# Identity products on TensorE ahead of 12 places of a two-block transformer kernel

## The chip, the cores and the metric

One core of a Trainium2 chip runs the whole program in one launch. The metric is the device time of that launch in microseconds (us), the median of several runs. All data are float32.

## The reference, cut to what matters

256 tokens of width 1024 pass through two layers of a first block (compressed, selected and windowed attention, a gated linear recurrence and a 31-tap convolution side by side) and then through one layer of a second block (latent attention, a chunked recurrent mixer, and a product-key expert layer).

```
for l in range(2):                                   # the first block
    proj = rms_norm(x, norm_g[l]) @ w_in[l]
    q, k_c, v_c, ..., u_lru, z_lru, glu_a, glu_b, z_conv = split(proj)
    y_nsa  = nsa_attention(rope(q), ..., compress: silu(blk @ cmp_w1) @ cmp_w2)
    y_lru  = rg_lru(u_lru, ...)
    y_conv = conformer_conv(glu_a, glu_b, ...)       # 31 taps, norm, @ w_pw2
    x = x + concat(y_nsa*silu(z_nsa), y_lru*silu(z_lru), y_conv*silu(z_conv)) @ w_out[l]
x = rms_norm(x, final_g)
# the second block: sh, sc, gt come from silu(c) @ w_ada
h = rmsnorm(x)*(1+sc1)+sh1;  x = x + gt1 * (concat(mla(h), mlstm(h)) @ w_out)
h2 = rmsnorm(x)*(1+sc2)+sh2
# experts: 8 heads x 16 rows of a table of 16384, chosen per token by two top-16 lists
x = x + gt2 * sum_k gelu(expert_u[e_k] . h2) * g_k * expert_v[e_k]
```

## The kernel before, in words

Every engine has its own instruction list, written out by hand, and events (semaphore counts) tie the lists together. TensorE runs through `first_tensor` for layer 0 and 1, `mix_tensor` (the mixers of the second block), and `peer_tensor` (the experts).

In `first_tensor` the projections come first. Then a loop over 20 steps interleaves 18 units of attention (16 heads of two token tiles, and two compressed units) with other products, listed by step in the table `BETWEEN`. The steps that matter here:

- step 3: `lru_gate` (needs `xc_ready` of VectorE), then `cmp` 0 and 1, the turned hidden rows of the key and value compression. ScalarE and VectorE make `hidT` from `cmp` 0.
- step 4: the scores of units 4 and 5, then `kcT` (`compressed_keys`, needs `hidT`), then `zlru` 2 (`by_feature`, 32 instructions), then `vc`. A float32 `pe.mm` shows as two MATMUL instructions in the trace.
- step 9: `mod` 0 (`modulation_turned`, 8 small instructions, needs ScalarE's copy of `ada` 0), then `pw` 0 and 2 (`pointwise`, needs `conv_act_ready`). Steps 11, 13 and 15 hold `mod` 1, 2 and 3.
- step 16 (`X_TURNED_AT`): after the unit's work, in layer 0 `gain_turned` and `x_turned` of the next layer's first tile, in layer 1 `block_turned` of the second block's first tile. Step 17: `out12` 1 1, 16 instructions.

Results go to eight PSUM banks. Five of them (0, 1, 2, 3, 7) are handed out in turn. `take` makes TensorE wait until the bank's last user has been read, and only then returns it:

```
    c.banks.rotate(0, 1, 2, 3, 7)                    # L3140, before both layers
        self.newest = (self.newest + 1) % len(self.rotation)
        bank = self.rotation[self.newest]
        if self.turns[bank]:
            self.pe.wait_ge(self.events.sem(f"bank{bank}_emptied"), self.turns[bank])
```

Between `cmp` 0 and `kcT` these take a bank, in this order: `cmp` 1, `turned` of unit 2, `scores` of units 4 and 5. VectorE tells that the bank of `cmp` 0 is empty with the second of its two instructions that write `hidT`. `pw` 0 takes the bank that `ada` 0 had. The banks 4 to 6 of the first block (`O`) are held for the values of the heads and are not handed out in turn; `O[0]` is bank 4.

In `peer_tensor`, `queries(k)` and `scores(k)` work on one head of the router, `list_spread(0)` gives the first list of expert rows to GpSimd, whose `fetch` (L3075) reads 4 rows' worth of tiles per batch from memory, 64 batches. `add` sums the fetched rows; the loop over `BATCHES` begins after `quarter_turned(0, 3)`. SyncE loads the second head's `w_pq` when `queries(0)` is done.

Of the kernel before, what the change touches and what calls it, by code (L numbers as in the profile page):

```python
# [14 lines left out]
P = 128  # L15
# [99 lines left out]
class Events:  # L115
# [25 lines left out]
    def at(self, name, *key):  # L141
        return self.sem(name), self.counted[(name, *key)] if self.counted else 1
# [111 lines left out]
class Banks:  # L254
# [11 lines left out]
    def take(self, *key):  # L266
# [5 lines that stand above are left out]
        self.turns[bank] += 1  # L272
        self.events.table[("bank of", *key)] = bank
        self.events.table[(f"bank{bank}_emptied", *key)] = self.turns[bank]
        return self.tiles[bank]
# [144 lines left out]
X_NORMED_AT, X_TURNED_AT = 15, 16  # L420
# [13 lines left out]
                      tell=c.banks.filled("xT", l, tt, half) if k == 3 else None)  # L434


def gain_turned(c, m, K, l):
    bank = c.banks.take("gT", l)
    c.pe.wait_ge(*c.at("gain_in", l))
    c.pe.turn(bank[:, 0:KT], m["grows"], K["ident"][0:KT, 0:KT], tell=c.banks.filled("gT", l))  # L440
# [93 lines left out]
def first_tensor(c, m, block, K, l):  # L534
    pe, at, take, filled = c.pe, c.at, c.banks.take, c.banks.filled
    ident, hT, mixT, cond = K["ident"], m["hT"], m["mixT"], m["cond"]
    qT, kT, vr, S, PT, O = m["qT"], m["kT"], m["vr"], m["S"], m["PT"], c.held
# [26 lines left out]
    bank = take("vec", l)  # L564
# [8 lines left out]
    if l == 0:  # L573
        bank = take("cond_vec")
# [14 lines left out]
    for ch in range(0, FT, 2):  # L589
        bank = take("qT", l, ch)  # L590
# [7 lines left out]
    bank = take("posT", l)  # L598
# [37 lines left out]

    def compressed_keys():
        bank = take("kcT", l)
        pe.wait_ge(*c.taken("cmp", l, 0))
        for g in range(KV):  # L640
            for half in range(2):
                pe.mm(bank[g * HD:g * HD + HD, 0:CMP_PAD], m["w2"][:, 0, half, :],
                      m["hidT"][:, 0, half, g * CMP_PAD:g * CMP_PAD + CMP_PAD], start=half == 0, stop=half == 1,
                      tell=filled("kcT", l) if (g, half) == (KV - 1, 1) else None)
# [8 lines left out]
    def scores(u, qt, i):  # L653

        nk = (qt + 1) * P
        banks = [take("scores", l, u + g) for g in range(KV)]
        for b in range(2):
            for g in range(KV):
                pe.mm(banks[g][:, b * T:b * T + nk], qT[g * HD:g * HD + HD, i, qt * P:qt * P + P],
                      kT[g * HD:g * HD + HD, b, 0:nk], tell=filled("scores", l, u + g) if b else None)  # L660
# [45 lines left out]
    def mixed(qt):  # L706
        bank = take("yT", l, qt)
        pe.wait_ge(*at("y_ready", l, qt))
        for ch in range(FT):
            pe.turn(bank[:, ch * P:ch * P + P], m["y"][:, ch * P:ch * P + P], ident,  # L710
                    tell=filled("yT", l, qt) if ch == FT - 1 else None)
# [7 lines left out]
    def pointwise(ch):  # L719
        view, landed = weight(m, l, "pw2")  # L720
        bank = take("pw", l, ch)
        pe.wait_ge(*at(*landed))
        pe.wait_ge(*at("conv_act_ready", l))
        for e in range(2):
            for k in range(FT):
                pe.mm(bank[:, e * T:e * T + T], view[:, k, (ch + e) * P:(ch + e) * P + P], m["conv_act"][:, k, :],
                      start=k == 0, stop=k == FT - 1, tell=filled("pw", l, ch) if (e, k) == (1, FT - 1) else None)
# [21 lines left out]

    def modulation_turned(j):  # L750
        bank = take("mod", l, j)
        pe.wait_ge(*c.taken("ada", l, j))
        for n in range(4):
            pe.mm(bank[:, 2 * n:2 * n + 2], cond["mod_rows"][:, n * P:n * P + P], K["fold"][:, 0:2],
                  tell=filled("mod", l, j) if n == 3 else None)
# [38 lines left out]
    pe.wait_ge(*c.taken("kT", l))  # L794
    pe.wait_ge(*c.taken("kvw", l, NT - 1))
    for step in range(STEPS):
        if step < len(UNITS):
            kind, qt, i, g = UNITS[step]
            if kind == "compressed":
                compressed_scores(step, qt)  # L800
            elif g == 0:
                scores(step, qt, i)
        between(step)
        if 1 <= step <= len(UNITS):
            kind, qt, i, g = UNITS[step - 1]
            if kind == "head":
                turned(step - 1, qt)
            else:
                compressed_turned(step - 1)
        if step >= 2:  # L810
            kind, qt, i, g = UNITS[step - 2]
            if kind == "head":
                values(step - 2, qt, i, g)
            else:
                compressed_values(step - 2, qt)
        if step == PER_TILE + 3:
            mixed(0)
        if l + 1 < DEPTH and step == X_TURNED_AT:
            gain_turned(c, m, K, l + 1)
            x_turned(c, m, K, l + 1, 0)  # L820
        if l + 1 == DEPTH and step in BLOCK_TURNS:
            block_turned(c, block, K, *BLOCK_TURNS[step])
# [824 lines left out]
def mix_tensor(c, m, K):  # L1647
    pe, at, take, filled = c.pe, c.at, c.banks.take, c.banks.filled
    ident, hTs = K["ident"], (m["hT_ctx"], m["hT"])
# [49 lines left out]
    bank = take("cqT")  # L1699
# [77 lines left out]
    tile.levels(0)  # L1777
    tile.lstm_scores(0)
    heads_turned(last - 1)
    pe.wait_ge(*c.taken("nope", last - 1))  # L1780
    pe.wait_ge(*c.taken("rope", last - 1))
    tile.att_scores(0, 1)
# [798 lines left out]
def peer_tensor(c, m, mix, K):  # L2581
# [130 lines left out]

    c.banks.leave(0)
    c.banks.leave(1)
    first.normed_turned()
    queries(0)
    scores(0)
    output_gate(mix, c, range(KT // 2, KT))
# [9 lines left out]
    quarter_turned(0, 2)  # L2728
    quarter_turned(0, 3)
    c.banks.rotate(2, 3, 7)  # L2730
    for g in range(BATCHES):
        route(routing_at(2 * g), "list")
        for step in second_tile_at(g):
            mixers(*step)
        one, *others = parts_of_batch(g)
        add(g, *one)
        for step in second_tile_at(g):
            mixers_after(*step)
        route(routing_at(2 * g), "scores", "weights", "queries")
        for more in others:  # L2740
            add(g, *more)
        route(routing_at(2 * g + 1), "scores", "weights", "queries")
# [367 lines left out]
def parts_of(nc, keep, A, out, counted):  # L3110
    c = Core(nc, counted)
    _, where = constants()
    x = nc.alloc_sbuf_tensor("x_sb", [P, NT, D], F32)[:]
    table = nc.alloc_sbuf_tensor("constants", [P, max(b for _, b in where.values())], F32)[:]
    K = {name: table[:, a:b] for name, (a, b) in where.items()}
    zeros = where["zeros"][0]
    K["masks"] = table[:, zeros + P:zeros + 3 * P].rearrange("p (d t) -> p d t", d=2)
    K["mask2"] = table[:, zeros:zeros + 2 * P]
    cond = c.cond = condition_memory(nc, keep)
    with ExitStack() as stack:  # L3120
        first = first_memory(nc, stack, cond)
    with ExitStack() as stack:
        second = second_memory(nc, stack)
        with ExitStack() as inner:
            mix = mix_memory(nc, inner, second, cond)
        with ExitStack() as inner:
            peer = peer_memory(nc, inner, second, cond)

    rows = A["x"].rearrange("b (t p) d -> p (b t) d", p=P)
    c.sp.load(x[:, 0, :], rows[:, 0, :], "x0_in", 0)  # L3130
    c.sp.load(table[:, 0:P], A["constants"][:, 0:P], "identity_in", 0)
    c.sp.load(first["grows"], A["norm_g"][0:1, :].rearrange("o (k p) -> (o k) p", p=P), "gain_in", 0)
    load_weights(c, first, A, 0, "q")
    c.sp.load(x[:, 1, :], rows[:, 1, :], "x1_in", 0)
    c.sp.load(first["posi"], A["positions"].rearrange("b (t p) -> p (b t)", p=P), "pos_in", 0,
              allow_slow_non_contiguous=True)
    c.sp.load(table[:, P:], A["constants"][:, P:], "constants_in", 0)
    c.pe.wait_ge(*c.at("identity_in", 0))

    c.banks.rotate(0, 1, 2, 3, 7)  # L3140
    for l in range(DEPTH):
        first_tensor(c, first, mix, K, l)
    first_vector_start(c, first, K)
    for l in range(DEPTH):
        first_sync(c, first, mix, K, A, l)
        first_vector(c, first, mix, K, x, l)
        first_scalar(c, first, mix, x, l)
    nc.all_engine_barrier()  # L3148
    held = c.banks.where(("mla", 0))
    c.banks.rotate(*(bank for bank in (0, 1, 2, 3, 5, 6, 7) if bank != held), held)  # L3150

    mix_tensor(c, mix, K)
    mix_sync(c, mix, K, A)
    mix_vector(c, mix, K, x)
    mix_scalar(c, mix, K, x)

    peer_tensor(c, peer, mix, K)
    peer_sync(c, peer, mix, A, x, out)
    peer_vector(c, peer, mix, K, x)
    peer_scalar(c, peer, mix, K, x)  # L3160
    peer_gpsimd(c, peer, A, x)
    return c.events.table
# [62 lines left out]
```

## Time and profile before

| | |
|---|---|
| runs of before | 1384.72, 1384.0 and 1392.3 us, median 1384.72 |
| the profiled execution | 1385.74 us, its span 1384.4 us |
| TensorE (PE) busy | 1019.2 us, 74% |
| VectorE (DVE) busy | 889.4 us, 64% |
| ScalarE (ACT) busy | 475.4 us, 34% |
| GpSimd (POOL) busy | 294.0 us, 21% |
| data moved | 391.12 MB, mean 283 GB/s |
| mean granted clock of TensorE | 0.85 of 2.4 GHz |

Times in the rows are us from the start of the span. "Granted clock" is the share of 2.4 GHz that TensorE got: 1.00 or 0.50 (1.2 GHz). In a timeline row, "[1.93 <-DVE mx L222]" is the idle time of the engine just before the group and what ended it. A row without a bracket had no such idle time.

### The profile page before, as it was taken

What the parts mean: (1) busy time and instruction counts of PE and PEld (TensorE: products, weight loads), DVE (VectorE), ACT (ScalarE), POOL (GpSimd) and SP (SyncE); (2) the same over time, 40 slices, a digit from 0 to 9 for tenths busy, and PEclk for the clock granted to TensorE, in tenths of its full rate; (3) what the DMA queues carried; (4) which work ended last, traced back from release to release, by engine and by line L of the source; (5) the groups of instructions that cost most, each with busy time, mean ns of one, the idle gap of its engine ahead of it and who ended that gap; (6) DMA issues with size and microseconds to landing.
All of it is one profiled execution on the core that took longest, in us unless ns stands there. A gap on an engine that the chain in (4) does not pass through costs nothing.

```text
span 1384.4 us, 17510 instructions
## 1 busy us (share of the span) xinstructions
PE 1019.2 (74%) x6217; PEld 589.7 (43%) x6217; DVE 889.4 (64%) x2281; ACT 475.4 (34%) x1312; POOL 294.0 (21%) x265
## 2 busy tenths in 40 slices
PE   7997999999799999998878686755443444442534
PEld 4776755477585555545544332332211222220200
DVE  5488543328855444845476898676777766877754
ACT  2013523101342431366257755532233222223321
POOL 0000000000000000000034445453433443442551
PEclk9998999999999989999999999886665666666655
DMA  8362364426337323125279999999999999999996
GB/s 303 130 223 92 134 231 137 182 73 232 140 111 276 107 93 125 71 87 218 99 288 426 425 426 427 426 425 426 426 427 426 427 426 425 427 426 425 427 427 279
DMA packets 56106, 391.12 MB, mean 283 GB/s; under 512 B 9931, under 2 KB 13055, under 8 KB 15955
## 3 DMA queue, kind: packets, MB, share of 16 engines
q0 software_dynamic: 37440, 268.45, 46.1%
q1 hardware_dynamic: 18578, 121.56, 23.8%
q8 instruction: 49, 0.80, 0.2%
q14 instruction: 39, 0.31, 0.1%
HBM read 387.89 MB, written 1.05 MB: 281 GB/s over the span
## 4 chain that ended last, share of the span: by engine, by line
DMA 30%; PE 13%; DVE 9%; ACT 4%; POOL 4%; issue 2%; ACTq 0%; DVEq 0%
DMA e_uv<-in_experts_dram,e_listed 27%; PE bank L169 12%; POOL e_uv L3075 4%; DVE e_uv L2869 3%; DMA e_uv<-in_experts_dram,e_listed_uv 2%; ACT e_diag L230 1%; ACT m_W L230 1%; ACT L230 1%; DMA m_w<-in_ada_dram 1%; PE bank L174 1%; DVE m_ctx L185 0%; ACT e_hT L230 0%; DVE m_W L185 0%; DVE e_h2q L197 0%; DMA e_w_pq<-in_w_pq_dram 0%
## 5 line engine op out<-in xcount | busy, mean ns | idle before, releaser
L3075 POOL DMA_INDIRECT e_uv<-in_experts_dram,e_listed x252 | 283.4, 1125 | 1055.4 <-DVE e_listed L202 824.3
L169 PE MATMUL bank<-e_uv,e_diag 128*32 128x512 f32 x1024 | 231.8, 895 | 303.1 <-ACT e_diag L230 303.1
L2869 DVE CUSTOM_DVE_ANT_0 e_uv<-e_uv,e_h2q 128x1024 f32<-128x1024 f32 x192 | 230.3, 1224 | 115.1 <-DMA e_uv<-in_experts_dram,e_listed 114.4
L169 PEld LDWEIGHTS bank<-e_uv,e_diag 128*32 128x32 f32 x1024 | 41.6, 141 | 426.6 <-ACT e_diag L230 336.3
L169 PE MATMUL bank<-hT,weights 128*128 128x256 f32 x640 | 146.8, 391 | 2.4 <-DVE hT L191 1.4
L169 PEld LDWEIGHTS bank<-hT,weights 128*128 128x128 f32 x640 | 124.8, 196 | 22.3 <-DVE hT L191 1.6
L230 ACT ACTIVATE e_act<-e_dot 128x4 f32<-128x4 f32 (+1 forms) x81 | 16.6, 205 | 283.5 <-DVE e_dot L2869 282.5
L169 PE MATMUL bank<-weights,hT 128*128 128x512 f32 (+1 forms) x256 | 103.0, 559 | 1.6 <-DMA weights<-in_layer_q_dram 1.6
L230 ACT ACT_TABLE_LOAD x79 | 101.4, 1283 | 6.2 <-PEq L3221 0.7
L197 DVE SCALAR_TENSOR_TENSOR conv<-ubuf,vec,conv 128x256 f32<-128x256 f32 x240 | 96.8, 479 | 0.6
L2869 DVE CUSTOM_DVE_ANT_0 e_uv<-e_uv,e_hT 128x1024 f32<-128x1024 f32 x64 | 77.0, 1224 | 28.5 <-DMA e_uv<-in_experts_dram,e_listed 28.4
L169 PE MATMUL bank<-weights,mixT 128*128 128x512 f32 x192 | 90.2, 625 | 2.0 <-DVE mixT L202 1.6
L169 PEld LDWEIGHTS bank<-e_hT,e_w_pq 128*128 128x128 f32 x512 | 64.3, 207 | 20.9 <-issue 19.0
L169 PEld LDWEIGHTS bank<-weights,hT 128*128 128x128 f32 x256 | 48.9, 194 | 49.6 <-issue 44.5
L169 PE MATMUL bank<-e_hT,e_w_pq 128*128 128x128 f32 x512 | 67.5, 294 | 2.5 <-ACT e_hT L230 2.4
L230 ACT ACTIVATE e_diag<-cond_mod_rows,e_act 128x32 f32<-128x32 f32 x256 | 63.1, 311 | 8.1
L230 ACT ACTIVATE cond_mod_rows<-constants,e_weight 128x32 f32<-128x32 f32 x256 | 61.3, 310 | 2.1
L169 PEld LDWEIGHTS bank<-weights,mixT 128*128 128x128 f32 x192 | 37.4, 200 | 47.9 <-issue 45.6
L185 DVE TENSOR_TENSOR x_sb<-bank,x_sb 128x512 f32<-128x512 f32 x16 | 11.1, 691 | 67.1 <-PE bank L169 67.1
L230 ACT ACTIVATE S<-S,mx 128x128 f32<-128x128 f32 (+1 forms) x64 | 29.1, 455 | 61.5 <-DVE mx L222 59.2
L169 PE MATMUL bank<-m_w,e_hT 128*128 128x464 f32 (+1 forms) x96 | 39.9, 568 | 1.2 <-PEq L3148 1.1
L234 ACT COPY PT<-bank 128x256 f32<-128x256 f32 (+2 forms) x36 | 16.4, 455 | 56.1 <-PE bank L174 53.4
(383 smaller groups left out, 1381.8 us busy)
## 6 DMA issues: line engine op xcount, KB each, us to landing
weights<-in_ada_dram SPq DMA_DIRECT2D x8, 2048.0 KB, 8.7
weights<-in_layer_out_dram SPq DMA_DIRECT2D x6, 2048.0 KB, 8.2
e_w_pq<-in_w_pq_dram SPq DMA_DIRECT2D x12, 1024.0 KB, 9.4
weights<-in_layer_cmp_dram SPq DMA_DIRECT2D x4, 2048.0 KB, 8.3
weights<-in_layer_q_dram SPq DMA_DIRECT2D x2, 2048.0 KB, 8.6
weights<-in_layer_kvc_dram SPq DMA_DIRECT2D x2, 2048.0 KB, 12.3
weights<-in_layer_gb_dram SPq DMA_DIRECT2D x2, 2048.0 KB, 15.2
weights<-in_layer_ga_dram SPq DMA_DIRECT2D x2, 2048.0 KB, 15.3
```

Source lines behind the costliest of these rows:

```text
L169: ins = self.engine.matmul(out, lhsT, rhs, start=start, stop=stop, **kw)
L174: ins = self.engine.transpose(out, a, ident)
L185: return self.mark(self.engine.tensor_tensor(out, a, b, op), tell)
L197: return self.mark(self.engine.scalar_tensor_tensor(out, a, s, b, op0, op1), tell)
L230: return self.mark(self.engine.activation(out, a, func, **kw), tell)
L234: return self.mark(self.engine.copy(out, a), tell)
L2869: dve.mark(c.nc.vector.tensor_tensor_reduce(u, u, h2q[tt][n], 1.0, 0.0, MUL, ADD, m["dot"][:, j:j + 1]), ("dots_set", g, c0) if n == c1 - ...
L3075: ins = c.nc.gpsimd.indirect_dma_start(out=to, out_offset=None, in_=rows, in_offset=bass.IndirectOffsetOnAxis(ap=of, axis=0))
```

## The change

A helper `kept_busy` multiplies the 128 by 128 identity by a constant block of 128 by 512 (the first 512 columns of the constants: the identity, zeros and two masks) into a given bank, a given number of times. Nothing reads the results. It is called at 12 places, each in TensorE's list alone; per layer of the first block these are 20 products, in the mixers 2, in the experts' start 4, and 6 just before the loop over the batches.

```diff
+def kept_busy(c, K, bank, times):
+    for _ in range(times):
+        c.pe.mm(bank[:, :], K["ident"], K["wide"])
...
     def compressed_keys():
         bank = take("kcT", l)
+        kept_busy(c, K, bank, 5)
         pe.wait_ge(*c.taken("cmp", l, 0))
...
         bank = take("pw", l, ch)
+        if ch == 0:
+            kept_busy(c, K, bank, 1)
         pe.wait_ge(*at(*landed))
         pe.wait_ge(*at("conv_act_ready", l))
...
         bank = take("mod", l, j)
+        kept_busy(c, K, bank, 2 if j == 3 else 1)
         pe.wait_ge(*c.taken("ada", l, j))
...
     for step in range(STEPS):
+        if step in (4, 16):
+            kept_busy(c, K, O[0], 2)
         if step < len(UNITS):
...
+        if step == 3:
+            kept_busy(c, K, O[0], 3)
         between(step)
...
+        if step == X_TURNED_AT:
+            kept_busy(c, K, O[0], 2)
         if l + 1 < DEPTH and step == X_TURNED_AT:
             gain_turned(c, m, K, l + 1)
...
     heads_turned(last - 1)
+    kept_busy(c, K, tile.values, 2)
     pe.wait_ge(*c.taken("nope", last - 1))
...
+    kept_busy(c, K, bank_q, 1)
     first.normed_turned()
+    kept_busy(c, K, bank_q, 3)
     queries(0)
...
     c.banks.rotate(2, 3, 7)
+    kept_busy(c, K, later.values, 6)
     for g in range(BATCHES):
...
+    K["wide"] = table[:, 0:4 * P]
```

## Rows read from the trace of the kernel before

**Rows 1.** Page, 40 slices: granted clock and GB/s
```profile
PEclk9998999999999989999999999886665666666655
...
GB/s 303 130 223 92 134 231 137 182 73 232 140 111 276 107 93 125 71 87 218 99 288 426 425 426 427 426 425 426 426 427 426 427 426 425 427 426 425 427 427 279
```

**Rows 2.** Windows, half-clock stretches: length, PE busy (instructions), clock, DMA share, GB/s
```profile
126.50:136.60 10.10, 6.31 (x21) 0.50 0.00 1
177.70:181.00 3.30, 3.30 (x9) 0.50 0.99 422
239.10:245.90 6.80, 6.41 (x12) 0.50 0.00 0
375.70:385.80 10.10, 6.52 (x22) 0.50 0.01 2
...
485.00:498.50 13.50, 11.49 (x38) 0.50 0.17 70
686.50:689.70 3.20, 3.20 (x16) 0.51 0.00 0
717.00:720.40 3.40, 3.01 (x8) 0.51 1.00 422
```

**Rows 3.** Timeline of PE, layer 0, steps 3 to 5
```profile
117.62 3.71 PE L169 MATMUL bank<-xc,bd 128*128 128x256 f32 x16 [1.93 <-DVE mx L222]
...
125.75 0.71 PE L169 MATMUL bank<-kT,qT 64*128 64x128 f32 x8 [1.41 <-ACT fc L230]
130.16 0.62 PE L169 MATMUL bank<-hidT,w 128*64 128x16 f32 x8 [3.69 <-DVE hidT L197]
130.91 10.01 PE L169 MATMUL bank<-hT,weights 128*128 128x256 f32 x32
...
141.76 7.12 PE L169 MATMUL bank<-hT,weights 128*128 128x256 f32 x32
```

**Rows 4.** Timeline of PE, layer 0, step 9
```profile
175.64 1.05 PE L169 MATMUL bank<-constants,cond_mod_rows 128*128 128x2 f32 x8 [0.36 <-ACT cond_mod_rows L234]
177.45 8.83 PE L169 MATMUL bank<-xn,weights 128*128 128x256 f32 x32 [0.76 <-DVE xn L197]
```

**Rows 5.** Timeline of PE, layer 0, steps 11 to 13
```profile
198.05 1.05 PE L169 MATMUL bank<-constants,cond_mod_rows 128*128 128x2 f32 x8
...
209.14 7.13 PE L169 MATMUL bank<-weights,mixT 128*128 128x512 f32 x16
216.11 0.60 PE L174 MATMUL bank<-constants,S 128*128 128x128 f32 x4
```

**Rows 6.** Timeline of PE, layer 0, steps 16 and 17
```profile
236.98 0.22 PE L174 MATMUL bank<-constants,grows 8*128 8x8 f32 x1
238.49 0.66 PE L174 MATMUL bank<-constants,xn 128*128 128x128 f32 x4 [1.29 <-DVE xn L191]
239.54 1.11 PE L174 MATMUL bank<-constants,xn 128*128 128x128 f32 x4 [0.39 <-DVE mx L222]
240.58 9.77 PE L169 MATMUL bank<-weights,mixT 128*128 128x512 f32 x16
```

**Rows 7.** Timeline of PE, layer 1, steps 16 and 17
```profile
486.78 2.08 PE L169 MATMUL bank<-kT,qT 64*128 64x256 f32 x8 [0.49 <-DVE pc L197]
...
492.40 1.97 PE L174 MATMUL bank<-constants,m_xn 128*128 128x128 f32 x8 [1.51 <-DVE m_xn L191]
494.16 9.19 PE L169 MATMUL bank<-weights,mixT 128*128 128x512 f32 x16
```

**Rows 8.** Timeline of PE, mixers, after heads_turned
```profile
627.32 1.96 PE L169 MATMUL bank<-m_knT,m_qnT 128*128 128x512 f32 x4 [0.52 <-DVE m_knT L202]
```

**Rows 9.** Timeline of PE, start of the experts, and the first sums
```profile
683.58 1.09 PE L174 MATMUL bank<-constants,m_W 128*128 128x128 f32 x8 [0.67 <-DVE m_W L191]
686.35 5.38 PE L169 MATMUL bank<-e_hT,e_w_pq 128*128 128x128 f32 x32 [1.68 <-ACT e_hT L230]
...
717.39 3.36 PE L169 MATMUL bank<-e_uv,e_diag 128*32 128x512 f32 x8 [5.69 <-ACT e_diag L230]
```

**Rows 10.** Timeline of POOL, its first fetch
```profile
705.63 1.08 POOL L3075 DMA_INDIRECT e_uv<-in_experts_dram,e_listed  x1 [705.19 <-DVE e_listed L202]
```

## The prediction

> **What bounds the kernel now.** I read the page's 40 slices first. Up to about 700 us the granted clock is near full and the memory traffic goes up and down; from there to the end the traffic stands at 425 to 427 GB/s [rows 1]. The fetches of the expert rows begin at 705.63 us, when VectorE has written the first list [rows 10], and what follows is bound by the memory. So the kernel has two parts. In the second, a faster TensorE buys nothing. In the first, everything that brings the first list forward or back moves the end by as much, one for one. TensorE is that part's bound: it is busy nearly all the time, and its waits are short.
>
> Next I read the granted clock in narrow windows and asked for TensorE's busy time in each stretch at half clock [rows 2]. Before the first fetch there are seven such stretches; six have their row, and the seventh, layer 1's step 9, repeats the second one (3.20 us busy). Busy time adds up to 6.31 + 3.30 + 6.41 + 6.52 + 3.20 + 11.49 + 3.20 = 40.4 us. At full clock it would be half, so 20.2 us (1.5%) is the most that a clock which never falls could give. That is little above 1%, which is about what a measurement of this kernel can tell from no change. The Trainium skill ("TensorE: Matmul & The Clock Gate", Part 1, What's actually happening) holds that the warm-up is under 1% of a typical span; the rows above allow 1.5% here, and by the page no more than 13.8 us could be won.
>
> **What one product costs.** A float32 product of 128 by 512 shows as two instructions. Sixteen such instructions take 216.11 - 209.14 = 6.97 us at full clock [rows 5], so a product costs 0.87 us, and 1.74 at half. The 52 products are 45 us of TensorE time. They pay only where they lie in a wait, or where they keep the clock up for work behind them. Each place is therefore a small balance: products x 0.87, less the waits they fill, less half of the busy time at half clock that they save.
>
> **Steps 3 and 4: three and two products.** Three take 2.6 us in a wait of 1.93, two take 1.74 us in a wait of 1.41 [rows 3]. They end 0.7 and 0.3 us late. Neither costs anything: behind them comes the wait of 3.69 us for `hidT`, which VectorE sets at its own pace (its queue of convolution taps), and TensorE merely arrives there later.
>
> **Step 4: five products at `kcT`.** This is the place that decides. They are meant for the 3.69 us wait, but look at where they stand: behind `take("kcT")`. Five banks go round, and four takes lie between `cmp` 0 and `kcT`, so `kcT` gets the bank of `cmp` 0. That bank is told empty by the very instruction that finishes `hidT`. So the 3.69 us are waited inside `take`, the line below it waits for nothing more, and the five products run after the wait, ahead of `kcT` and `zlru`. They delay both, and do so at half clock if the clock has fallen meanwhile.
>
> Has it? The five products of steps 3 and 4 end at about 126.1 us, the scores at 126.8, and then TensorE is idle until 130.16, some 3.4 us. In the rows the clock fell 1.9 us after work ended at 237.2 [rows 2, 6] and 5.3 us after it ended at 711.7 [rows 2, 9]. Between these ends I take that it falls, by the nearer one. How soon does it come back? Dense work brought it back after 3.3 us at 686.35 and 3.0 at 717.39 [rows 2, 9]; after 130.16 it took 6.5, with small products first [rows 2, 3]. I take 3.2 us, since five products are dense from the start. Then 3.2 / 1.74 = 1.84 products run at half clock and 3.16 at full (2.75 us), 5.95 us in all. `kcT` adds 0.75 us (130.91 - 130.16) and `zlru`, at full clock, 7.12 as its twin at 141.76 does. It ends at 143.97 us instead of 130.91 + 10.01 = 140.92, 3.05 us late. TensorE is dense from here on, so nothing absorbs it. Bounds: clock never down, 130.16 + 4.35 + 0.75 + 7.12 = 142.38, 1.5 us late; clock back after 6.5 us, 3.74 products at half and 1.26 at full, 7.6 us, 4.7 late. Layer 1 is alike [rows 2]. Two layers: 6.1 us lost (3 to 9.4).
>
> The Trainium skill (same page, Part 1) says that the point at which the clock changes differs from run to run of one kernel, since it depends on where the chip's own count stands when work arrives. No row of this single execution can show that. By it the loss at `kcT` would be 1.5 us in some executions and 3 in others, which is the first rival below.
>
> **Step 9, `mod` 0 and `pw` 0.** Two products, 1.74 us, in waits of 0.36 + 0.76 [rows 4]: 0.6 late. Both stand before their waits: `take` for `pw` waits for the bank of `ada` 0, which `mod` 0 has already waited for. If the clock holds, 3.30 / 2 = 1.65 us are saved [rows 2]. Gain 1.0 us per layer, 2.0 in all. If the clock falls all the same, the loss is up to 1.5 per layer.
>
> **Steps 11 and 13, `mod` 1 and 2.** No wait before them, and the clock is full there [rows 5]: four products over two layers, 3.5 us lost.
>
> **Steps 15 to 17.** Six products, 5.2 us: two at `mod` 3, two before the scores of unit 16, two before the turns. In layer 0 they stand against waits of 1.29 + 0.39 and 6.41 / 2 = 3.2 us of clock [rows 2, 6], 4.9: loss 0.3. VectorE's `xn` moves back by the first two products only, so the wait for it is swallowed whole. In layer 1 the same six stand against 0.49 + 1.51 us of waits and 11.49 / 2 = 5.7 us of clock [rows 2, 7], 7.7: gain 2.5.
>
> **Mixers.** Two products in a wait of 0.52 [rows 8], 1.2 us late. TensorE has later waits that take this up, but the maximum, exponential and turn of the first head hang on these scores. I take 0.5 lost, between 0 and 1.2.
>
> **Start of the experts.** One and three products, 3.5 us, in waits of 0.67 + 1.68, so 1.1 late; clock saved 3.20 / 2 = 1.6 [rows 2, 9]. `queries(0)` ends 0.5 us sooner, and with it the load of the next `w_pq`, which `queries(1)` awaits. Gain 0.5.
>
> **Before the loop.** Six products, 5.2 us, in the wait of 5.69 [rows 9]. They cost nothing, and the 1.5 us of clock behind them gains nothing, as the fetches are already running at the memory's rate.
>
> **Sum.** -6.1 + 2.0 - 3.5 - 0.3 + 2.5 - 0.5 + 0.5 = -5.4 us. No DMA issue of SyncE or GpSimd is passed; all loads hang on TensorE's events and shift with them. The profiled execution took 1385.74 us (span 1384.4), 1 us over the median; the same shift gives 1391.1 there and 1390.1 against the median of 1384.72.
>
> **Rivals.**
>
> 1. The clock stays full through the wait at `kcT`, because steps 3 and 4 are now dense up to 126 us. For it: the 5.3 us it lasted after 711.7. Against it: 1.9 us after 237.2. It gives back 2 x 1.55 = 3.1 us: 1387.0.
>
> 2. Faster: the bank for `kcT` is free early, and the five products do lie in the wait. It decides whether they begin by 126.8: they would end at 131.2, 1.0 late, and `zlru` saves 2.9 us, a gain of 1.9 per layer in place of a loss of 3.05: 1384.7 + 5.4 - 9.9 = 1380.2. Against it stands the count of banks, which I have no reason to doubt. Some slack that I don't see behind the added 3.5 us of steps 11 and 13 would work the same way.
>
> 3. The clock falls anyway at step 9 or at steps 15 to 17, as one or two products are too few. Each miss costs 1.6 to 5.7 us and slows the products as well: 1393 to 1402.
>
> 4. The change doesn't do what it says: products of an identity with mostly zeros don't hold the clock. Then all seven stretches stay. At `kcT` 5 x 1.74 = 8.7 us are lost per layer; at step 9 1.5 per layer; steps 11 and 13 3.5; steps 15 to 17 some 5 and 8; the rest 3.5: about 40 us, 1425. Nothing in the rows speaks for it, since the clock followed how busy TensorE was.
>
> **How the numbers follow.** Forecast 0.58, first rival 0.18, second 0.10, third 0.09, fourth 0.05. The bounds of the two `kcT` terms (3.1 up, 3.3 down) and of step 9 and the mixers make 1386 to 1396 of the forecast. With part of the second rival the range is 1382 to 1396. All but the fourth and the top of the third lie within 1% (1370.9 to 1398.6): within 1% 0.88; slower by more 0.08; faster by more 0.04, for gains that I can't name, as the ceiling is 1.5%.
>
> **What the profile after would show.** The wait for `hidT` stands before the first of five identity products, not behind them, and `kcT` starts 4.4 to 7.6 us after it. `pw` 0, the turns of step 16 and `queries(0)` run at clock 1.00. Products at steps 11 and 13 have no idle time around them. The first fetch is at about 711 us instead of 705.63, and from there to the end the time is unchanged. I'm wrong if the products at `kcT` begin before `hidT` is set, if the fetch comes before 704 us, or if the part behind it changes by over 1 us.

## The result and the profile after

The changed kernel takes 1393.98 us in the median of its runs beside 1384.72 us for the kernel before. The ratio is 1.0064 with a 95% interval of 1.0049 to 1.0080, so some 9 us are lost (0.0064 x 1384.72 = 8.9). The forecast was a loss of 5.4 us, a ratio of 1.0039, which lies outside the interval; the time itself lies inside the stated range of 1382 to 1396. The profiled execution of the changed kernel took 1397.14 us with a span of 1395.8; the one of the kernel before took 1385.74 us, with a span of 1384.4.

First the page of the changed kernel: granted clock and memory rate in 40 slices.

```profile
PEclk9999999999999999999999989875676776667655
...
GB/s 301 150 200 91 121 241 136 179 64 235 144 75 295 99 116 131 64 91 211 106 301 379 426 426 426 426 423 380 415 426 426 426 426 426 427 426 425 427 427 295
```

Two things are to be seen against [rows 1]. The clock row has nines in its first 23 slices: the dips in the first part are gone. And the memory rate, which stood at 425 to 427 GB/s from the slice behind the first fetch almost to the end, now has dips: 379 in the 22nd slice, 380 and 415 in the 28th and 29th.

The windows at half clock ahead of the first fetch (length, busy time of PE, PEld, DVE, ACT and POOL, clock, DMA share, GB/s) are three, where the kernel before had seven (six of them in [rows 2]):

```profile
127.80:134.40 6.60, 5.30 (x7) 2.21 (x8) 5.49 (x24) 1.58 (x6) 0.00 (x0) 0.50 0.01 1
383.80:387.10 3.30, 3.30 (x5) 1.35 (x4) 2.81 (x14) 0.99 (x4) 0.00 (x0) 0.50 0.00 0
571.60:574.90 3.30, 3.30 (x5) 1.22 (x5) 2.83 (x8) 0.42 (x1) 0.00 (x0) 0.51 1.01 432
```

TensorE is busy for 11.9 us at half clock instead of 40.4. So the products do hold the clock. The next lines, TensorE's timeline in layer 0, show what is paid for it:

```profile
124.99 0.71 PE L169 MATMUL bank<-kT,qT 64*128 64x128 f32 x8
129.10 7.25 PE L169 MATMUL bank<-constants 128*128 128x512 f32 x10 [3.39 <-DVE hidT L197]
136.28 0.42 PE L169 MATMUL bank<-hidT,w 128*64 128x16 f32 x8
136.62 7.17 PE L169 MATMUL bank<-hT,weights 128*128 128x256 f32 x32
143.64 0.55 PE L169 MATMUL bank<-w,hid_rep 128*128 128x64 f32 x4
...
180.82 7.07 PE L169 MATMUL bank<-xn,weights 128*128 128x256 f32 x32
...
245.72 1.09 PE L174 MATMUL bank<-constants,xn 128*128 128x128 f32 x8
246.65 7.03 PE L169 MATMUL bank<-weights,mixT 128*128 128x512 f32 x16
```

The wait for `hidT` stands in front of the ten instructions of the five products, and `kcT` (`hidT,w`) starts 7.2 us after it. Ahead of `pw` and of the turns of `xn` no wait is left, and both run at full clock, 7.07 us for `pw` where [rows 4] have 8.83.

Two rows tell how the time divides. GpSimd's first fetch:

```profile
709.47 1.09 POOL L3095 DMA_INDIRECT e_uv<-in_experts_dram,e_listed  x1 [709.03 <-DVE e_listed L202]
```

It was at 705.63 in [rows 10], so this profile has 3.8 us more in the first part. Behind the fetch the kernel before took 1384.4 - 705.63 = 678.8 us, this one 1395.8 - 709.47 = 686.3: 7.5 us more in a part of which the prediction had said that its time is unchanged. These lines, TensorE's 128 turns of `h2q` just behind the first fetch, are where it begins:

```profile
711.81 0.86 PE L169 MATMUL bank<-constants,e_hT 128*32 128x128 f32 x24
712.97 0.43 PE L169 MATMUL bank<-constants,e_hT 128*32 128x128 f32 x5 [0.30 <-issue]
713.72 0.42 PE L169 MATMUL bank<-constants,e_hT 128*32 128x128 f32 x3 [0.32 <-issue]
714.43 0.27 PE L169 MATMUL bank<-constants,e_hT 128*32 128x128 f32 x1 [0.29 <-issue]
...
725.17 5.42 PE L169 MATMUL bank<-constants 128*128 128x512 f32 x12
730.52 1.91 PE L169 MATMUL bank<-e_uv,e_diag 128*32 128x512 f32 x8
```

The turns run from 711.81 to 725.17, 13.4 us. In the kernel before they took 3.74. No semaphore is waited for. After 24 of them only a handful come every 0.7 us, with "issue" between, as if TensorE got no instructions (the profile doesn't say so). The six products come behind that and end at 730.5, the first sums follow, and the buffers come free late. GpSimd stands for 12.8 us until TensorE has worked on them, and the rate falls:

```profile
732.71 1.95 POOL L3095 DMA_INDIRECT e_uv<-in_experts_dram,e_listed  x1 [12.83 <-PE bank L169]
```

The pair of profiles thus holds 1395.8 - 1384.4 = 11.4 us of difference where the medians hold 9. Whether the 7.5 us are the change's was the first question for the experiments.

### The profile page after: what moved, and what is told of

Its sections match the earlier page's. It is cut to its first block, busy times and chain, and to the rows that moved or that the text cites. A ratio compares the mean times of both kernels' runs of the same rounds, so it can differ in the third digit from the quotient of the medians.

```text
span 1395.8 us, 17715 instructions
## 1 busy us (share of the span) xinstructions
PE 1055.5 (76%) x6321; PEld 600.9 (43%) x6321; DVE 887.4 (64%) x2281; ACT 475.5 (34%) x1312; POOL 305.4 (22%) x265
## 4 chain that ended last, share of the span: by engine, by line
PE 19%; DMA 17%; DVE 13%; ACT 4%; issue 4%; another core or an unknown queue 3%; POOL 2%; ACTq 0%; DVEq 0%
PE bank L169 18%; DMA e_uv<-in_experts_dram,e_listed 14%; DVE e_uv L2889 5%; POOL e_uv L3095 2%; DMA e_uv<-in_experts_dram,e_listed_uv 2%; ACT e_diag L230 1%; DVE e_hot L185 1%; DVE e_rest L2820 1%; ACT m_W L230 1%; DMA m_w<-in_ada_dram 1%; ACT L230 1%; PE bank L174 0%; DVE m_ctx L185 0%; ACT e_h2q L230 0%
## 5 line engine op out<-in xcount | busy, mean ns | idle before, releaser
L3095 POOL DMA_INDIRECT e_uv<-in_experts_dram,e_listed x252 | 294.8, 1170 | 1055.3 <-DVE e_listed L202 826.3
L169 PE MATMUL bank<-hT,weights 128*128 128x256 f32 x640 | 141.0, 380 | 2.2 <-DVE hT L191 1.4
L169 PEld LDWEIGHTS bank<-hT,weights 128*128 128x128 f32 x640 | 120.8, 190 | 20.2 <-DVE hT L191 1.6
L169 PE MATMUL bank<-weights,mixT 128*128 128x512 f32 x192 | 85.3, 597 | 2.0 <-DVE mixT L202 1.6
L169 PE MATMUL bank<-constants 128*128 128x512 f32 x104 | 54.8, 657 | 7.1 <-DVE hidT L197 7.1
L2816 DVE MAX8 e_sv<-cond_mod_rows 128x8 f32<-128x128 f32 x32 | 9.4, 295 | 66.3 <-ACT cond_mod_rows L234 53.9
```

Source lines behind the costliest of these rows:

```text
L169: ins = self.engine.matmul(out, lhsT, rhs, start=start, stop=stop, **kw)
L2816: dve.mark(c.nc.vector.max(out_v[:, 0:8], values))
L3095: ins = c.nc.gpsimd.indirect_dma_start(out=to, out_offset=None, in_=rows, in_offset=bass.IndirectOffsetOnAxis(ap=of, axis=0))
```

## The experiments

Twelve kernels ran, four to a chip, on three chips; the kernel before ran beside them on each. First fetch, and the part behind it (span less first fetch), are those of one profile of each kernel. "Turns" are the 128 turns of `h2q`.

| kernel | chip | half clock ahead of the fetch, us | first fetch | behind | turns | ratio to before (95%) |
|---|---|---|---|---|---|---|
| before | first | 51.2 | 705.6 | 678.8 | 3.74 | |
| changed | first | 13.7 | 709.5 | 686.3 | 13.4 | 1.0064 (1.0049 to 1.0080) |
| e1_kct_tiny | A | 13.7 | 703.6 | 678.1 | 3.74 | 1.0016 (0.9999 to 1.0032) |
| e2_kct_ahead | A | 0 | 698.6 | 678.8 | 3.74 | 0.9987 (0.9970 to 1.0003) |
| e3_stream_only | A | 44.4 | 697.9 | 678.5 | 3.74 | 0.9992 (0.9971 to 1.0014) |
| e4_pad_256 | A | 6.8 | 709.1 | 677.6 | 3.74 | 1.0069 (1.0043 to 1.0094) |
| e5_no_11_13 | B | 0 | 694.7 | 684.2 | 13.2 | 0.9979 (0.9959 to 1.0000) |
| e6_only_in_waits | B | 3.4 | 694.1 | 684.8 | 12.7 | 0.9954 (0.9938 to 0.9970) |
| e7_change_again | B | 10.2 | 708.5 | 684.6 | 13.4 | 1.0070 (1.0043 to 1.0097) |
| e8_before_again | B | 41.0 | 698.3 | 688.6 | 13.8 | one execution |
| e9_no_15_17 | C | 23.9 | 694.7 | 677.5 | 3.74 | 0.9962 (0.9944 to 0.9980) |
| e10_no_9 | C | 0 | 692.9 | 680.6 | 3.74 | 0.9961 (0.9943 to 0.9980) |
| e11_only_kct | C | 20.5 | 695.4 | 679.2 | 3.74 | 0.9966 (0.9950 to 0.9983) |
| e12_fetch_late | C | 0 | 701.1 | 679.1 | 3.74 | 1.0004 (0.9986 to 1.0023) |

**e1_kct_tiny: without the wide products at `kcT`.**

```
         bank = take("kcT", l)
-        kept_busy(c, K, bank, 5)
+        feed_only(c, K, bank, 5)     # 128 by 32 times 128 by 2
```

> The changed kernel, with the five wide products at kcT of each layer replaced by five of 32 by 2 elements, so that TensorE's stream of instructions keeps its length. Theory (the products run behind the wait for hidT and are the largest loss): after hidT the changed kernel needed 7.25 + 0.42 + 7.17 us up to vc, and the kernel before 0.75 + 10.01; without the wide products it is about 10.8 again instead of 14.5, 3.7 to 4 us a layer. The first fetch comes at about 702 instead of 709.5 us, and the whole takes 7.5 us less than the changed kernel, about 1386 to 1387. Rival (something else ends last behind kcT, as VectorE's hid_rep): the first fetch stays above 707 us. On the part behind the first fetch (686.3 us against 678.8 before): if it comes from the position of TensorE's instructions in the stream, it stays at 685 to 687; if it comes from the six wide products ahead of the loop it stays too.

The median is 1382.42 us beside 1378.73 for the kernel before. TensorE's timeline:

```profile
130.41 0.69 PE L169 MATMUL bank<-constants 128*32 128x2 f32 x10 [3.39 <-DVE hidT L197]
131.03 0.62 PE L169 MATMUL bank<-hidT,w 128*64 128x16 f32 x8
131.59 9.79 PE L169 MATMUL bank<-hT,weights 128*128 128x256 f32 x32
141.21 0.55 PE L169 MATMUL bank<-w,hid_rep 128*128 128x64 f32 x4
```

From the end of the wait to `vc` (`w,hid_rep`) it takes 10.8 us, where the changed kernel took 14.5: 3.7 us in layer 0. In layer 1 it is 10.6 and 13.6, so 3.0. Both are near the 3.7 to 4 that were expected. The first fetch is at 703.6 instead of 709.5, and at 709.1 in e4_pad_256 on the same chip. By the ratios, 0.0053 x 1378.73 = 7.3 us come back compared with e4_pad_256. So the five products at `kcT` are the largest loss. The part behind the fetch is 678.1, which already speaks against the stream's length as a cause: it was kept, and the turns have no gaps.

**e2_kct_ahead: the five one line earlier.**

```
+        kept_busy(c, K, O[0], 5)
         bank = take("kcT", l)
-        kept_busy(c, K, bank, 5)
```

> The changed kernel, with the five products at kcT written into O[0] one line earlier, ahead of take(kcT), so that they lie in the wait for hidT. The stream of instructions has the same length. Theory: they fill the 3.4 to 3.7 us wait and end some 1 us behind it; zlru runs at full clock, 7.1 us. Up to vc some 3 us sooner than with the kernel before minus 1 for the overhang, so 1.9 a layer better than without products, and 5.5 to 6 a layer better than the changed kernel: first fetch at 698 to 699 us, the whole at 1382 to 1384 with the part behind the fetch as in the changed kernel. Rival (the products delay something else by as much): first fetch above 704 us.

```profile
126.78 4.56 PE L169 MATMUL bank<-constants 128*128 128x512 f32 x10
131.26 0.42 PE L169 MATMUL bank<-hidT,w 128*64 128x16 f32 x8
131.61 7.17 PE L169 MATMUL bank<-hT,weights 128*128 128x256 f32 x32
138.62 0.55 PE L169 MATMUL bank<-w,hid_rep 128*128 128x64 f32 x4
```

The wait is gone from the row, and `zlru` takes 7.17 us. The first fetch comes 5.0 us before that of e1_kct_tiny and 10.5 before that of e4_pad_256. In the whole first part no stretch at half clock is left. Even so, the median is 1378.01 beside 1378.73, no gain that can be measured: all products together cost about as much as they save.

**e3_stream_only and e4_pad_256: the length of the instruction stream.** The first adds 23 small products (32 by 2) ahead of `take("kcT")` in each layer of the kernel before, 184 instructions, as many as the change adds ahead of the turns; the second adds nine more a layer to the changed kernel.

```
+        feed_only(c, K, O[0], 23)    # e3; e4: 9, in the changed kernel
         bank = take("kcT", l)
```

> The kernel before, with 23 products of 32 by 2 elements in each layer ahead of take(kcT), in the wait for hidT: 46 products, 184 instructions, as many as the change adds ahead of the turns of h2q. No wide product is added, so the clock does as before. Theory (the position of the instruction stream is what costs 7.5 us behind the first fetch): up to the first fetch as before (705.6, at most 1 later), but the 128 turns of h2q take 8 us or more instead of 3.74 and show idle gaps that no semaphore ends, the memory's rate falls below 400 GB/s in a slice behind 710 us, and the part behind the fetch is 4 to 8 us longer: 1389 to 1393. Rival (the loss behind the fetch comes from the wide products or from when the fetches begin): no gaps, the part behind the fetch 678.8, the whole 1384 to 1386.

> The changed kernel, with nine products of 32 by 2 elements more in each layer ahead of take(kcT): 72 instructions, so that what is added ahead of the turns of h2q is 256 instructions. The instruction fetches of TensorE's queue in the trace move 16 KB each, 256 instructions of 64 bytes. Theory of the stream position: the turns of h2q again stand as in the kernel before, take 3.7 to 4 us without gaps, and the part behind the first fetch falls back from 686.3 to about 679; the whole at 1387 to 1389. Rival: it stays at 685 to 687, the whole at 1394.

My theory fell. With the shift alone the turns take 3.74 us, the part behind is 678.5, and the time is unchanged (0.9992). In e4_pad_256 the gaps are gone, as foreseen, but they are gone in e1_kct_tiny and e2_kct_ahead too, which keep the changed kernel's stream. And the ratio of e4_pad_256, 1.0069, is no better than that of the change with gaps. The first fetch of e3_stream_only also brought something unforeseen: 697.9 us, although the clock was down for 44 us on the way, against 51 in [rows 2]. The 705.6 of the first profile was not typical of the kernel before. The times say so too: on chip A 4 of its 30 executions took 1385.4 to 1386.3 us and on chip C 5 of 34 took 1385.5 to 1386.2, as that profile did (1385.74), with medians of 1378.7 and 1379.0. The kernels with the filled wait had none above 1379.7 on A (e2_kct_ahead) and 1377.9 on C (e9 to e11). No profile shows one of these long executions on A or C, so what happens in them is not shown.

**e7_change_again and e8_before_again: both kernels once more, unchanged, on one chip.**

> The changed kernel itself, once more, to see whether the loss behind the first fetch is its own. Theory A (it belongs to single executions): the part behind the first fetch is 677.6 to 678.8 us, the 128 turns of h2q take 3.74 us without gaps, and the ratio to the kernel before is below that of the first comparison, near 1.0055 (first fetch 4 us later, plus what the executions differ by). Theory B (it belongs to the kernel): part behind at 685 to 687 us, gaps of 0.3 to 1.1 us between groups of turns, ratio 1.006 to 1.009.

> The kernel before itself, one look, for the spread of its first part: the first fetch stood at 705.6 us in the first profile and at 697.9 in the profile of the kernel with 23 small products a layer. Theory: the spread is that of single executions, by where the clock falls, and by the chip, so the first fetch lies between 697 and 706 us and the part behind it at 678 to 679. If the first fetch is at 705 us or more on this chip too, the small products bought 7 us.

This shows that the 7.5 us need no product of the change. The kernel before, on chip B, has its first fetch here and its turns right behind it:

```profile
698.29 1.09 POOL L3075 DMA_INDIRECT e_uv<-in_experts_dram,e_listed  x1 [697.85 <-DVE e_listed L202]
```

```profile
700.63 0.95 PE L169 MATMUL bank<-constants,e_hT 128*32 128x128 f32 x25
701.88 0.42 PE L169 MATMUL bank<-constants,e_hT 128*32 128x128 f32 x4 [0.30 <-issue]
702.63 0.42 PE L169 MATMUL bank<-constants,e_hT 128*32 128x128 f32 x4 [0.34 <-issue]
704.10 0.27 PE L169 MATMUL bank<-constants,e_hT 128*32 128x128 f32 x1 [1.04 <-issue]
...
709.82 4.64 PE L169 MATMUL bank<-constants,e_hT 128*32 128x128 f32 x81 [0.78 <-issue]
717.66 1.07 PE L169 MATMUL bank<-e_uv,e_diag 128*32 128x512 f32 x2 [3.20 <-ACT e_diag L230]
```

It has the same gaps without a product of the change, and 688.6 us behind the fetch. On chip B all four kernels have them, on A and C none of eight. Theory B is refuted as a statement about the change, and theory A in its wording too: in these profiles the gaps go with the chip rather than with the execution. Two things leave it open whether that is the whole of it: the first pair, one profile without gaps and one with, and the times of the kernel before on B, which spread from 1378.0 to 1393.2 us. They fall out of the comparison, as far as both kernels bear them alike: the change's ratio is 1.0070 on B and 1.0064 on the first chip, and with nine small products more a layer (e4_pad_256) it is 1.0069 on A.

The second finding is in the clock. The windows of the kernel before on chip B:

```profile
118.50:121.80 3.30, 3.30 (x9) 2.64 (x8) 3.30 (x9) 2.78 (x9) 0.00 (x0) 0.50 0.95 400
128.80:135.50 6.70, 5.52 (x20) 4.43 (x21) 5.59 (x25) 1.58 (x6) 0.00 (x0) 0.50 0.00 1
...
364.30:367.60 3.30, 3.30 (x10) 2.59 (x9) 3.26 (x10) 2.80 (x10) 0.00 (x0) 0.50 0.94 400
...
480.30:490.40 10.10, 7.47 (x28) 5.50 (x28) 6.65 (x24) 7.41 (x14) 0.00 (x0) 0.50 0.16 67
```

The same kernel, other places: with four more stretches the busy time at half clock is 33.8 us instead of 40.4, and 6.6 of it, at 118.5 and 364.3, lies ahead of the wait for `hidT`, which swallows it. What counts is 27.2, half of which is 13.6 us, against 20.2 in the first profile: 6.6 us, most of the 7.3 us by which the first fetches differ. Against this profile, on one chip, the changed kernel's first fetch (708.5) is 10.2 us late, and the medians differ by 9.8 (1395.76 and 1385.97). The two profiled executions differ by 6.2 only, as the part behind is 684.6 us in the one and 688.6 in the other: what the gaps cost varies by 4 us.

**e5_no_11_13 and e6_only_in_waits: what the other products cost.**

```
-        kept_busy(c, K, bank, 2 if j == 3 else 1)
+        if j in (0, 3):                                # e5
+            kept_busy(c, K, bank, 2 if j == 3 else 1)
...
-    kept_busy(c, K, tile.values, 2)                    # e6, as well
...
-    kept_busy(c, K, later.values, 6)                   # e6, as well
```

Both have the five ahead of `take("kcT")`.

> The kernel with the five kcT products ahead of the wait, and without the one product at mod 1 and at mod 2 of each layer (steps 11 and 13): four products and 16 instructions fewer. Theory: no wait stands before them and the clock is full there without them, so four times 0.87 = 3.5 us come back, the first fetch at about 695 instead of 698.6 us and the whole 3.5 us below the kernel with the products ahead (1378.0 beside 1378.7 of the kernel before on that chip), so a ratio to the kernel before of about 0.996. Rival: these products keep the clock up for steps 11 to 15; then a stretch at half clock appears between 185 and 235 us or 435 and 480 us, and what comes back is under 2 us.

> The last kernel, also without the two products in the mixers and the six ahead of the loop. Theory: the mixers' two cost 0 to 1.2 us, so the first fetch comes 0.5 us sooner than in the last kernel; the six cost nothing and gain nothing, and the part behind the first fetch stays at 677.6 to 678.8 us. The whole at a ratio of about 0.9955 to the kernel before. Rival for the six (they hold up the first sums, which hold up the buffers of the next fetches): the part behind the first fetch is 0.3 us shorter or more. Rival the other way (the half clock that they were to avert costs): it is over 0.5 us longer.

The first fetch comes at 694.7 and 694.1: 3.9 us sooner without `mod` 1 and 2 (e2_kct_ahead had 698.6), and 0.6 more without the mixers' two. First fetches carry the execution's own scatter: ahead of the first product of any kernel, TensorE stood at the same instruction at 109.8 to 111.5 us in the fourteen profiles. Measured where the products stood, `mod` 1 and 2 cost 1.7 us a layer, 3.4 in all. The clock stays full without the four products. Behind the fetch 684.2 and 684.8 say nothing of the six, on a chip with gaps where the kernel before itself had 688.6. The ratio of e6_only_in_waits, 0.9954 with its interval below 1, is the first that beats both kernels.

**e9_no_15_17, e10_no_9 and e11_only_kct: which products earn something.** From e6_only_in_waits, the first drops the six of steps 15 to 17, the second the two of step 9. The third keeps only those of steps 3 and 4 and the five ahead of `take("kcT")`.

```
-        if step in (4, 16):                            # e9, e11
+        if step == 4:
...
-        if step == X_TURNED_AT:                        # e9, e11
-            kept_busy(c, K, O[0], 2)
...
-        if ch == 0:                                    # e10, e11
-            kept_busy(c, K, bank, 1)
```

(With them go the products at `mod` 3 in e9 and e11, at `mod` 0 in e10 and e11, and the four at the experts' start in e11.)

> The kernel with products in the waits alone (five ahead of the kcT wait, none at mod 1 and 2, in the mixers and ahead of the loop), without the six products of steps 15 to 17 as well. Before the run it stands at a first fetch of 694.1 us and a ratio to the kernel before of 0.9954. Theory of the prediction (the six lose 0.3 us in layer 0 and win 2.5 in layer 1): the first fetch comes 2.2 us later, 696.3. What the comparison of the changed kernel with the second profile of the kernel before shows (they lose 1.2 us in layer 0 and win 1.3 in layer 1): first fetch unchanged, 693.5 to 694.8, with stretches at half clock back behind 237 and 480 us.

> The same kernel with products in the waits alone, without the two products of step 9 (mod 0 and pw 0) in each layer. Theory of the prediction (the clock falls there and costs 1.65 us, the products cost 0.6 more than their waits, so they win 1.0 a layer): first fetch 2.0 us later, 696.1, with a stretch at half clock at 173 to 178 us and 415 to 428 us. Rival (with the clock up since kcT it doesn't fall at step 9 any more): no such stretch, and the first fetch up to 1.2 us sooner.

> The kernel before with the products of steps 3 and 4 and the five ahead of the kcT wait alone, ten a layer. Theory: the wait for hidT is filled, zlru runs at full clock, and this is most of what the products can win: against the second profile of the kernel before (first fetch 698.3 us) 3.1 us in layer 0 and, by layer 1's smaller part at half clock, 1 to 2 there; first fetch at 694 to 695, ratio 0.996 to 0.997. Rival (it takes the products of all places to hold the clock, since a gap later loses it anyway): first fetch above 697 us, ratio over 0.9985.

The windows of e9_no_15_17 show the clock down again where the products are gone:

```profile
229.50:239.50 10.00, 10.00 (x34) 7.00 (x34) 5.59 (x22) 6.97 (x15) 0.00 (x0) 0.50 0.24 102
475.20:488.70 13.50, 11.92 (x42) 8.58 (x41) 8.41 (x27) 9.37 (x19) 0.00 (x0) 0.50 0.20 84
```

Half of 21.9 us is 11.0 us of clock, and in layer 1 a wait of 1.51 us is back; the twelve products cost 10.4. So they should win some 2 us. The first fetch is only 0.6 us later and the ratio is 0.9962, but the first fetch holds more than that. At the same place of the program, here layer 1, from step 15 to the end of `out12`, the rows are, first of e6_only_in_waits and then of e9_no_15_17:

```profile
473.80 1.07 PE L169 MATMUL bank<-kcT,qT 64*128 64x16 f32 x16
...
492.19 0.60 PE L174 MATMUL bank<-constants,S 128*128 128x128 f32 x4
```

```profile
473.00 1.07 PE L169 MATMUL bank<-kcT,qT 64*128 64x16 f32 x16
...
493.69 0.60 PE L174 MATMUL bank<-constants,S 128*128 128x128 f32 x4
```

With the six it takes 18.4 us, without them 20.7: they win 2.3. In layer 0 it is 18.7 and 18.2, so they lose 0.5. That is 1.8 us won, near the 2.2 of the prediction. It doesn't arrive at the first fetch, since e9_no_15_17 was 0.3 us ahead from the start and e6_only_in_waits had a stretch at half clock in the mixers, worth 0.7.

In e10_no_9 the clock doesn't fall at step 9 at all:

```profile
172.93 1.05 PE L169 MATMUL bank<-constants,cond_mod_rows 128*128 128x2 f32 x8 [0.36 <-ACT cond_mod_rows L234]
174.74 7.15 PE L169 MATMUL bank<-xn,weights 128*128 128x256 f32 x32 [0.76 <-DVE xn L197]
```

Both waits of [rows 4] are back, and `pw` still takes 7.15 us instead of 8.83. The first fetch is at 692.9, the earliest of all. At the place itself the two products cost 0.4 us a layer; the rest of the 1.2 us to e6_only_in_waits is elsewhere. Whether the clock falls at step 9 when only these two are dropped from the changed kernel, where the five stand behind the wait, was not tried. e11_only_kct, with ten products a layer and nothing else, has 0.9966. The three ratios and that of e6_only_in_waits lie within each other's intervals, so which is best stays open; all four beat the kernel before by 0.3 to 0.5%, and e11_only_kct shows that the filled wait alone gives most of it (0.34% beside 0.38 to 0.46).

**e12_fetch_late: e6_only_in_waits with the fetches held back.**

```
+            if g == 0 and n == 0:
+                pool.wait_ge(*c.full("h2q", 0, 3, 1))
```

> The kernel with products in the waits alone, and GpSimd waits ahead of its first fetch of expert rows until the last 64 turns of h2q are done, so that these 128 turns of TensorE run while the memory is nearly idle. The first fetch is 5.5 us late and everything behind it. On a chip where the turns stand with gaps (four of the last four profiles): if the traffic of the fetches is what starves TensorE of instructions, the 128 turns take 3.74 us without gaps, the part behind the first fetch falls from about 684.5 to some 679 or below, and the total comes out within 1 us of the kernel without this wait. If the gaps come from something else, as the place of the code, they stay, and the total is 5 us or more longer. On a chip where the other three kernels show no gaps it tells nothing but the 5.5 us.

Chip C shows no gaps in any kernel, so this tells only the price of the late fetch: 701.1 instead of 694.1 us, 679.1 behind, ratio 1.0004. What makes TensorE stand in the turns stays open.

## Why the forecast held in sign and place, and was too small

**`kcT`: right, a little small.** The step had -6.1 us for two layers between 3 and 9.4. The order in the trace is as described, since `take` does the waiting. The five products take 7.2 us in layer 0 of the first profile, and 6.2 in its layer 1 and in both layers of e7_change_again, where 5.95 were forecast. Counted from the end of the wait to `vc`, e7_change_again loses 3.4 and 3.8 us against e8_before_again, 7.2 in all, since the kernel before spends less of this place at half clock there (5.52 and 4.64 us busy, not 6.31 and 6.52). In the first pair of profiles it is 4.0 and 2.9, 6.8 in all. Between e4_pad_256 and e1_kct_tiny, on one chip, the first fetch moved by 5.5 us. The clock was down at this place in both layers in both profiles of the changed kernel, so the first rival (1387.0) was out. So was the second: the bank isn't free early. What it would have been worth, 9.9 us against the forecast, was measured all the same: e2_kct_ahead, with the five in the wait, has its first fetch 10.5 us before e4_pad_256.

**`mod` 1 and 2: right.** 3.5 us forecast, 3.4 measured at the place. **Mixers: right**, 0.5 forecast, and the first fetch 0.6 sooner without them. **Before the loop**: no row contradicts the zero, and none here is sharp enough to prove it.

**The gains: this is the term that was mis-sized.** TensorE's instructions stand in the same order in all kernels, so two traces can be laid side by side and the shift of one against the other read place by place (plus is later):

| place, both layers unless said | forecast | changed - before, first pair | e7 - e8, chip B |
|---|---|---|---|
| ahead of the first product | 0 | -1.1 | -0.8 |
| steps 3 and 4, to `vc` | +6.1 | +6.8 | +7.2 |
| from `vc` to the end of `pw`, step 9 | -2.0 | -2.6 | -0.8 |
| to step 15, with `mod` 1 and 2 | +3.5 | +3.4 | +3.4 |
| steps 15 to 17, layer 0 | +0.3 | 0.0 | +1.9 |
| steps 15 to 17, layer 1 | -2.5 | -2.5 | -1.2 |
| mixers and start of the experts | 0 | -0.3 | +0.4 |
| first fetch | +5.4 | +3.8 | +10.2 |

Against the execution that the prediction had read, each term is within 0.7 us of its forecast, and without the first line, which lies ahead of every product, the places add up to 4.9 us. So the balance of products, waits and clock is sound. What failed is the step from that one execution to the kernel: "Step 9 ... Gain 1.0 us per layer, 2.0 in all" came out as 0.8, and steps 15 to 17, from which the sum had 2.2 us, lost 0.7. In the second profile of the kernel before there is no stretch in layer 1's step 9 or at `queries(0)`, and layer 0's step 17 has 3.3 us instead of 6.8; where the clock doesn't fall, there is nothing to win. The prediction's ceiling of 20.2 us was 13.6 there. With `kcT` at +7.2 the places add up to 10.9 us, 10.2 at the first fetch, where 5.4 were forecast; the medians of this chip differ by 9.8 and those of the first by 9.

The Trainium skill ("TensorE: Matmul & The Clock Gate", Part 1) was cited for saying that the point where the clock changes differs from run to run of one kernel. The two profiles of the kernel before agree: the first stretch starts at 126.5 us in one and at 118.5 in the other. I had used it to price one rival and not to doubt the gains, where it mattered more. Its other statement, under 1% of a typical span for the warm-up, fits the second profile (13.6 us on the path are 0.98%) and not the first (20.2 us, 1.5%).

**The part behind the fetch.** "I'm wrong if the part behind it changes by over 1 us." In the pair of profiles it changed by 7.5, and the sentence would have condemned the forecast wrongly: the kernel before has 678.8 and 688.6 itself. The two accidents of the pair, an unlucky first part in the profile of before (7 us) and the gaps in that of after (7.5 us), nearly cancelled in the total and hid each other: 11.4 us beside 10.2 for the first part on chip B.

**The other rivals.** The clock didn't fall at step 9 or at steps 15 to 17 in the changed kernel (third rival), and the fourth was out with the first window: an identity with mostly zeros does hold the clock. 1394 lies in the third rival's band without its mechanism.

## What to carry to other kernels

A filler that is meant for a wait pays only if it is issued ahead of the instruction that really waits. Look for that one in the code: here it was the bank's `take`, one line above the wait that names the awaited result, and moving the five products over it turned 10 us of loss into none. Sum what the fillers cost and what the waits and the clock cost at each place on its own: the same six products a layer, at steps 15 to 17, won 2.5 us against one execution of the kernel before and lost 0.7 against another. So size gains from a fallen clock by at least two executions of the kernel before; one of them may stand 7 us off in its first part. And compare two traces place by place, since the first fetch alone mixes the place in question with everything ahead of it.

## What the hardware showed beyond that

TensorE can stand without waiting for anything that the profile shows. In five profiles of fourteen (one on the first chip, all four on chip B) the 128 small turns took 12.7 to 13.8 us instead of 3.74, always from about the 25th turn on (the first gap ends 3.5 to 3.6 us after GpSimd's first fetch), with a handful of instructions every 0.7 us. It came again at 937 us in the first profile of the changed kernel, at 936 in e7_change_again and at 929 in e8_before_again, in turns of the same kind. The memory rate fell to 379 and 380 GB/s in the changed kernel's slices just behind these places; ahead of the first of them GpSimd had waited 12.8 us for buffers. The packets of 16 KB that the trace has in an instruction queue don't explain it: near the first fetch they took 0.9 to 1.2 us in the changed kernel and in e8_before_again, which have gaps, and 1.3 to 1.4 us in the first profile of the kernel before, which has none. The Trainium skill ("Runtime: NRT & Kernel Launch", Instruction fetch mechanics) says that instructions come in blocks of 16 KiB, with a cost that is mostly hidden. On chips A and C no row speaks against it. On chip B the part behind the first fetch is 6 to 10 us longer, and whether that is a cost of fetching instructions, no run shows. Padding the stream was tried on chip A alone, where there was nothing to mend.
